# Two products instead of three: high and low activation side by side in one 512-column product, and wider output chunks

## The chip, the cores and the metric

The kernel runs on one core of a Trainium2 chip. The metric is the time of one execution on the device in microseconds (us). Three runs of the kernel before took 2255.21, 2258.01 and 2260.10, with a median of 2258.01.

The engines are TensorE (PE: matrix products; its weight loads are listed as PEld), VectorE (DVE), ScalarE (ACT), GpSimd (POOL), and SyncE (SP), which issues most transfers. TensorE reads SBUF and writes PSUM.

## The reference

Two transformer blocks for one sequence of 256 tokens with 2048 features, in float32. The first block has two layers, the second one layer:

```
for l in range(2):                                  # first block
    h = x @ w_in[l]                                 # 2048 x 8278: queries, keys, values, gates, index
    y_fox = softmax(q k / sqrt(d) + decay, causal) v * silu(gate)      # 6 heads
    y_dsa = softmax over the 64 keys chosen by an index score * silu(gate)   # 6 heads, rotary q and k
    y_mem = softmax(q k_mem) v_mem * silu(gate)     # 4 heads, keys and values from mem @ w_mem_kv[l]
    x = layer_norm(ALPHA * x + concat(y) @ w_out[l])
a = rms_norm(x); proj = a @ w_in_2                  # second block
mixed = concat(attention(q, k, v), conv(u)) @ w_out_2
x = x + rms_norm(mixed)
f = square(relu(rms_norm(x) @ w_ff1)) @ w_ff2       # 2048 -> 8192 -> 2048
x = x + rms_norm(f)
```

Nearly all of the arithmetic is in the products with weights. The kernel makes each in three parts: with w = wh + wl and x = xh + xl, where the h parts are rounded to the type float32r and the l parts are the remainders, it adds wh xh, wh xl and wl xh.

## The kernel before, in words

**Blocks.** All weights stream through SBUF as 734 blocks of 128 partitions by 1024 values (512 KB; some of 512 values). A block g has a place in a ring of four (`RING`): SyncE loads it into `raw`, ScalarE rounds it into `high` (`round_block`, L804), and VectorE or GpSimd writes the remainder into `low` (`low_part`, L449). GpSimd takes every second block in slots 40 to 133 of each layer and all of slots 18 to 83 of block 2. TensorE multiplies the block in `weight_block` (L589 to L618, the product at L617). ScalarE may round block g once TensorE is done with block g - 4.

**Chunks.** `plan` (L91) groups the blocks into chunks, each of which sums over all K-tiles of 128 rows into one of two pairs of PSUM banks (`acc`). Chunks alternate between the pairs, so a chunk waits until the result of the one before the last was read (`acc_released`, L528). There are two kinds. A *flipped* chunk holds 256 output features; the weights are the stationary operand and the activation of 256 tokens moves, so the result has features on the partitions. It takes four blocks of four K-tiles. An unflipped chunk moves the weights and keeps the activation stationary; it has 512 columns (eight blocks of two K-tiles) or 256 columns. Flipped are mk (keys of the memory, 4 chunks in all), mg, fg, fq, fk, mq, iq, dg, dq and dk (26 chunks in each layer), val, gt, q2 and k2 (16 chunks in block 2), and f1 (32). A narrow flipped chunk, nar, is apart in its own bank. Unflipped are the values, the output projections o (in each layer), oa and ob, and f2. The output columns are cut by `COLS` (L76): two chunks of 512 and four of 256. ob sums over 10 K-tiles in five blocks a chunk, two K-tiles in a block.

**Slots.** Each engine goes through the same list of slots, one per block. `slots` (L372) first serves block b, then the side work of slot b - 3 (`LEAD`). The side work is written out by slot number: `ends(b, kinds)` (L423) names the chunk whose last block was b - 1, and then the result is read. ScalarE reads keys, queries, values and gates (`copied_out`, L897; its copy of keys is L913) and the relu (`relu_square`, L1064). VectorE reads what is rotated (`rope`, L1127: first product L1137, parts L1140, last add L1143), the second block's val, gt, q2 and k2 (L1490), and the output sums (`add_residual`, `mix_sum`, `ff_sum`).

**Attention.** `SCORES` and `SCORES2` (L177 to L180) give the slot of each head. In slot b TensorE makes the scores (L641 for memory heads, L644 and L645 for others), VectorE the maximum (L1179 for memory heads), and ScalarE the exponentials. In slot b + 1 VectorE takes the reciprocal of the sums (L1197) and ScalarE the probabilities (L835). In slot b + 2 TensorE transposes them (L655), in b + 3 it multiplies by the values. Within a slot, VectorE's rotation stands ahead of its attention work. The top-k choice takes eight rounds in slots 90 to 97 on VectorE. The depthwise convolution of block 2 is spread over slots 18 to 80, four steps a slot on VectorE (L1462).

**The feed-forward part.** Four rounds, each with 8 f1 chunks and then the f2 chunks; the last three are a loop. The first two f1 chunks of the first round run interleaved, block by block. After the last f2 chunk come its sum (L1416), squares (L894), the root, the gain (L1438) and the last additions, and four transfers out.

Of the kernel before, what the change touches and what calls it, by code (L numbers as in the profile page):

```python
# [54 lines left out]
NQ = 4  # L55
# [20 lines left out]
COLS = [(0, 512), (512, 512), (1024, 256), (1280, 256), (1536, 256), (1792, 256)]  # L76
NC = len(COLS)

# [12 lines left out]
def plan(a):  # L91
# [82 lines left out]
BLOCK2, BLOCK2_SLOTS = LAYER0 + DEPTH * LAYER_SLOTS, 122  # L174
# [3 lines left out]
SCORES |= {62 + 2 * h: ("mem", h) for h in range(HM)}  # L178
# [5 lines left out]
GLU_AT = (17, 25, 41, 49)  # L184
# [27 lines left out]
def build(nc, a, out):  # L212
    by, chunk_at, acc_users = plan(a)
    with ExitStack() as ctx:
# [9 lines left out]
        xh = sb("xh", [P, KT, S], F32R)  # L224
        xl = sb("xl", [P, KT, S], F32R)

        with nc.sbuf_tensor("yhf", [P, KT, S], F32) as yhf:
            pass
        yh = sb("yh", [P, KT, S], F32R)
        with nc.sbuf_tensor("ylf", [P, KT, S], F32) as ylf:  # L230
            pass
        yl = sb("yl", [P, KT, S], F32R)
# [6 lines left out]
        consts = sb("consts", [P, N_CONST])  # L239
        params = sb("params", [P, N_PARAM])  # L240
        small = sb("small", [P, 384])
# [19 lines left out]
        def const(name, *dims):  # L261
            return cut(consts, CONST[name][0], *(dims or (CONST[name][1] - CONST[name][0],)))
# [5 lines left out]
        ident, mask, upto = const("ident"), const("mask"), const("upto")  # L268
# [20 lines left out]
        def mixed_cols(n):  # L289

            col, width = COLS[n]
# [23 lines left out]
        def vec(name, n):  # L315
            sm[name] = small[:, sm_at[0]:sm_at[0] + n]
            sm_at[0] += n
            assert sm_at[0] <= 384
# [16 lines left out]
            v_ready g_ready rot_ready nar_ready flog_in flog_e flog_ln logf_ready wi_ready warm_done ikt_ready slope_ready  # L335
# [7 lines left out]
         logf_ready, wi_ready, warm_done, ikt_ready, slope_ready, cum_ready, decay_ready, rel_ready, rel_used,  # L343
# [18 lines left out]
        def accs(c):  # L362

            b = 2 * (c.acc % 2)
            return acc[:, b:b + 2, 0:256 if c.width == 256 else CW]

# [42 lines left out]
        def sums(kind, *at):  # L409

            return {"o": 0, "oa": 2 * NC, "ob": 2 * NC + 4, "f2": 3 * NC + 4}[kind] + NC * sum(at[:-1]) + at[-1] + 1
# [43 lines left out]
        def _(pe):  # L455
# [72 lines left out]
            def acc_released(c, turn):  # L528
# [22 lines left out]
                else:  # L551
                    pe.wait_ge(sum_ready, NC * turn + sums(*k))
# [36 lines left out]
            def weight_block(g, turn=0):  # L589
# [10 lines left out]
                vh, vl = (yh, yl) if k[0] in ("mk", "mv", "o", "oa", "ob", "f2") else (xh, xl)  # L600
# [4 lines left out]
                for t in range(c.nk):  # L605
                    kt = c.kt0 + c.nk * i + t
                    first, last = i == 0 and t == 0, i == c.n - 1 and t == c.nk - 1
                    for s in range(len(outs)):
                        at = slice(s * P, min(s * P + P, c.width if c.flipped else S))
                        if c.flipped:  # L610
                            products = ((wh[:, t, at], vh[:, kt, :]), (wh[:, t, at], vl[:, kt, :]),
                                        (wl[:, t, at], vh[:, kt, :]))
                        else:
                            products = ((vh[:, kt, at], wh[:, t, :]), (vh[:, kt, at], wl[:, t, :]),
                                        (vl[:, kt, at], wh[:, t, :]))
# [182 lines left out]
        def _(act):  # L798
# [128 lines left out]
            def mem_side(b):  # L927
                name = ends(b, "mk", "mv")
# [10 lines left out]
            for l in range(DEPTH):  # L939
                g0 = LAYER0 + LAYER_SLOTS * l  # L940

                def layer_side(b, l=l, g0=g0):
                    name = ends(g0 + b, "mv", "fq", "fk", "mq", "fv", "dv", "mg", "fg", "dg")
                    if name:
                        copied_out(name)
# [51 lines left out]
            def block2_side(b):  # L997
                name = ends(BLOCK2 + b, "val", "gt", "v2")
# [44 lines left out]
                if b in (98, 103, 108, 113, 118):  # L1043
                    n = (b - 98) // 5
                    act.wait_ge(sum_ready, sums("ob", n))
                    squares(mixed_cols(n), n)
# [4 lines left out]
            squares(mixed_cols(NC - 1), NC - 1)  # L1051
# [27 lines left out]
            def ff_side(b, q, turn=0):  # L1079
                name = ends(FF0 + FF_SLOTS * q + b, "f1")  # L1080
# [13 lines left out]
            for n in range(NC):  # L1094
                act.wait_ge(sum_ready, sums("f2", NQ - 1, n))
                squares(mixed_cols(n), n)
# [4 lines left out]
        def _(dve):  # L1101
# [14 lines left out]

            def low_block(g, turn=0):
# [9 lines left out]
            def rope(k):  # L1127
# [7 lines left out]
                acc_done(c)  # L1135
# [27 lines left out]
            def max_of_scores(l, kind, h):  # L1163
                j = job_no(l, kind, h)
                r = 2 * (j % 4)
                if kind == "fox":
# [3 lines left out]
                                                  in1=mask[:, 0:P], op0=ALU.subtract, op1=ALU.add))  # L1170
                    dve.scalar_tensor_tensor(out=nfox[:, P:3 * P], in0=t[:, 0:S], scalar=cum[:, 1, h:h + 1],
                                             in1=mask[:, P:3 * P], op0=ALU.subtract,
# [61 lines left out]
            def mem_side(b):  # L1234
                if 8 <= b < 24 and b % 2 == 1:
# [25 lines left out]
            for l in range(DEPTH):  # L1261
# [16 lines left out]
                def layer_side(b, l=l, g0=g0):  # L1278
                    name = ends(g0 + b, "iq", "dq", "dk", "o")
# [37 lines left out]
                    if b == TOPK_AT + TOPK // 8 + 1:  # L1317

                        for s, n in ((0, P), (1, S)):
# [3 lines left out]
                                                   mask[:, P * s:P * s + n], ALU.add))  # L1323
# [28 lines left out]
                def select_round(r, l=l):  # L1352

                    both = ((0, P), (1, S))
                    if r == 0:
# [4 lines left out]
                        for s, n in both:  # L1360
                            step(dve.tensor_tensor(iscore[:, s, 0:n], iscore[:, s, 0:n], mask[:, P * s:P * s + n],
# [48 lines left out]
            def ff_sum(name, turn):  # L1410
# [3 lines left out]
                for s in range(ST):  # L1414
                    rows = mixed_cols(n)[:, s, :]
# [3 lines left out]
                dve.wait_ge(sum_ready, NC * turn + sums(*name))  # L1419

            def mix_sum(name):
# [5 lines left out]
                else:  # L1427
                    rows = mixed_cols(name[1])
# [288 lines left out]
```

## Time and profile before

| | |
|---|---|
| runs: lowest, median, highest | 2255.21, 2258.01, 2260.10 us |
| profiled execution: its time | 2256.79 us |
| its span in the trace | 2255.0 us |
| mean granted TensorE clock | 0.991 |
| TensorE products: busy | 2201.1 us (98%) |
| TensorE weight loads: busy | 2088.9 us (93%) |
| VectorE: busy | 1231.1 us (55%) |
| ScalarE: busy | 1058.1 us (47%) |
| GpSimd: busy | 392.3 us (17%) |
| moved by DMA | 395.32 MB, mean 175 GB/s |

Products are pipelined, and the duration shown for one is from its start to its modelled end, so neighbours overlap; the distance between the starts of two is what one costs in a stream. All times of the rows are from one profiled execution and counted from the start of its span.

### The profile page before, as it was taken

Reading aid. Unit: us, or ns where it says so; the run is one execution under the profiler, and the core shown is the slowest. Engines: PE = TensorE matmul, PEld = TensorE weight load, DVE = VectorE, ACT = ScalarE, POOL = GpSimd, SP = SyncE. Lnnn points to the kernel's source line nnn. Section 1 sums busy time; section 2 is a strip of 40 time slices with the busy share of each in tenths; the row PEclk is TensorE's granted clock in tenths of the full one; section 3 lists DMA queues with packets and bytes.
Section 4 is the critical chain, followed back from the end, with each engine's and each line's share of the span. In section 5 each row is a group of like instructions: output and inputs, shape, how many; then the busy total and the mean of one; then the engine's idle time right before and its main releaser. Section 6 shows DMA issues by size and latency. Waiting matters only on the chain.

```text
span 2255.0 us, 38841 instructions
## 1 busy us (share of the span) xinstructions
PE 2201.1 (98%) x16028; PEld 2088.9 (93%) x16028; DVE 1231.1 (55%) x1774; ACT 1058.1 (47%) x1438; POOL 392.3 (17%) x176
## 2 busy tenths in 40 slices
PE   8999999999999999999989999989999999999997
PEld 7999998998889999998979999789899999989987
DVE  4443346765565335855577555665544454444455
ACT  4444454444454554444454445556434434533543
POOL 0000323331000233332007875000000000000000
PEclk9999999999999999999999999999999999999999
DMA  8666545655666555555656655556666665665663
GB/s 272 192 179 184 153 137 163 179 154 181 189 170 179 153 148 167 162 166 167 188 159 197 187 162 166 165 164 181 190 184 183 186 188 170 185 189 175 181 193 124
DMA packets 346186, 395.32 MB, mean 175 GB/s; under 512 B 20336, under 2 KB 295920, under 8 KB 345120
## 3 DMA queue, kind: packets, MB, share of 16 engines
q1 hardware_dynamic: 344368, 383.20, 57.0%
q0 software_dynamic: 1648, 9.64, 1.1%
q8 instruction: 132, 2.16, 0.4%
q14 instruction: 38, 0.31, 0.0%
HBM read 390.70 MB, written 2.10 MB: 174 GB/s over the span
## 4 chain that ended last, share of the span: by engine, by line
PE 94%; DVE 3%; ACT 2%; issue 1%; DMA 0%; DVEq 0%; SPq 0%; ACTq 0%
PE acc L617 88%; ACT high L804 1%; PE tb L559 1%; DVE low L449 1%; PE obank L677 1%; PE sbank L645 1%; PE tb L655 1%; PE sbank L701 0%; PE sbank L617 0%; PE sbank L641 0%; PE sbank L644 0%; PE obank L678 0%; ACT x_nat L972 0%; DVE x_nat L1445 0%; DVE work L1143 0%
## 5 line engine op out<-in xcount | busy, mean ns | idle before, releaser
L804 ACT ACTIVATE high<-raw 128x1024 fp32r<-128x1024 f32 (+1 forms) x734 | 765.9, 1045 | 908.2 <-PE acc L617 891.3
L449 DVE TENSOR_TENSOR low<-raw,high 128x1024 fp32r<-128x1024 f32 (+1 forms) x574 | 709.0, 1236 | 740.6 <-ACT high L804 738.7
L617 PE MATMUL acc<-xh,high 128*128 128x256 f32 x3200 | 919.3, 287 | 10.1 <-DVE low L449 6.9
L617 PE MATMUL acc<-xh,low 128*128 128x256 f32 x3200 | 907.2, 283 | 0.0
L617 PE MATMUL acc<-xl,high 128*128 128x256 f32 x3200 | 907.0, 283 | 0.0
L617 PEld LDWEIGHTS acc<-xh,high 128*128 128x128 f32 x3200 | 615.6, 192 | 13.6 <-DVE low L449 7.3
L617 PEld LDWEIGHTS acc<-xl,high 128*128 128x128 f32 x3200 | 615.6, 192 | 1.1
L617 PEld LDWEIGHTS acc<-xh,low 128*128 128x128 f32 x3200 | 615.5, 192 | 0.0
L449 POOL TENSOR_TENSOR low<-raw,high 128x1024 fp32r<-128x1024 f32 x160 | 384.7, 2407 | 778.7 <-ACT high L804 778.6
L617 PE MATMUL acc<-high,yh 128*128 128x256 f32 (+1 forms) x1384 | 451.7, 326 | 1.5 <-DVE work L1426 1.0
L617 PE MATMUL acc<-high,yl 128*128 128x256 f32 (+1 forms) x1384 | 448.8, 324 | 0.0
L617 PE MATMUL acc<-low,yh 128*128 128x256 f32 (+1 forms) x1384 | 448.7, 324 | 0.0
L617 PEld LDWEIGHTS acc<-high,yh 128*128 128x128 f32 x1384 | 263.4, 190 | 24.2 <-DVE work L1426 1.4
L617 PEld LDWEIGHTS acc<-high,yl 128*128 128x128 f32 x1384 | 263.4, 190 | 21.4
L617 PEld LDWEIGHTS acc<-low,yh 128*128 128x128 f32 x1384 | 263.5, 190 | 20.5
L617 PE MATMUL acc<-high,xh 128*128 128x512 f32 (+1 forms) x320 | 115.8, 362 | 0.7 <-issue 0.7
L617 PE MATMUL acc<-low,xh 128*128 128x512 f32 (+1 forms) x320 | 112.4, 351 | 0.0
L617 PE MATMUL acc<-high,xl 128*128 128x512 f32 (+1 forms) x320 | 112.3, 351 | 0.0
L1462 DVE SCALAR_TENSOR_TENSOR tb<-work,params,tb 128x256 f32<-128x256 f32 x232 | 93.4, 481 | 0.0
L617 PEld LDWEIGHTS acc<-high,xh 128*128 128x128 f32 x320 | 61.5, 192 | 11.0 <-issue 2.7
L617 PEld LDWEIGHTS acc<-high,xl 128*128 128x128 f32 x320 | 61.4, 192 | 8.1
L617 PEld LDWEIGHTS acc<-low,xh 128*128 128x128 f32 x320 | 61.6, 193 | 7.2
(204 smaller groups left out, 1348.8 us busy)
## 6 DMA issues: line engine op xcount, KB each, us to landing
raw<-in_w_in SPq DMA_DIRECT2D x336, 512.0 KB, 3.7
raw<-in_w_ff SPq DMA_DIRECT2D x256, 512.0 KB, 3.8
raw<-in_w_out SPq DMA_DIRECT2D x86, 512.0 KB, 3.9
raw<-in_w_mem_kv SPq DMA_DIRECT2D x32, 512.0 KB, 5.0
raw<-in_w_out SPq DMA_DIRECT2D x20, 256.0 KB, 3.0
x_nat<-in_mem SPq DMA_DIRECT2D x4, 512.0 KB, 7.8
x_nat<-in_x POOLq DMA_DIRECT2D x4, 512.0 KB, 6.3
yhf<-in_ln_gain POOLq DMA_DIRECT2D x2, 1024.0 KB, 5.1
```

The lines of the kernel that those rows point to most:

```text
L449: eng.tensor_tensor(part(low, g), part(raw, g), part(high, g).bitcast(F32), ALU.subtract).then_inc(ready, 1)
L559: ins = pe.transpose(t[:, dt * S + s * P:dt * S + s * P + P], src[:, s, first + dt * P:first + dt * P + P], ident)
L617: ins = pe.matmul(outs[s], stationary, moving, start=first and n == 0, stop=last and n == 2)
L645: ins = pe.matmul(sbank[:, S:2 * S], q[:, h, P:S], k[:, h, :], start=True, stop=True)
L655: ins = pe.transpose(t[:, n * P:n * P + P], sc[:, j % 2, s, kk * P:kk * P + P], ident)
L677: pe.matmul(obank[:, 0:S], v0, t[:, 0:S], start=True, stop=False)
L804: act.activation(part(high, g), part(raw, g), ACT.Copy).then_inc(high_ready, 1)
L1462: ins = dve.scalar_tensor_tensor(out=cv[:, ct, :] if tap == TAPS - 1 else sums_at, in0=src, scalar=w, in1=sums_at, op0=ALU.mult, op1=ALU.add)
```

## The change

In a flipped chunk the first two products, wh with xh and wh with xl, become one of 512 columns. For it `xh` and `xl` (and `yh` and `yl`) are two halves of one tensor, and the moving operand takes K-tile kt of both, in two runs of 256. The result fills a whole bank: the left half holds wh xh, the right half wh xl. The third product, wl with xh, adds to the right half. When the chunk has ended, ScalarE copies the right half of both banks to SBUF (`cross_out`), VectorE adds the copy to the left half in PSUM (`fold`), and only then the result is read. ScalarE's readers of flipped chunks move to the slot after; VectorE's stay in the slot of the fold, but f1's remainder (L1571) moves by two. The memory heads move from slots 62 to 68 to slots 64 to 70, and the gating of the convolution moves by one slot.

Besides, two of the 256-wide output chunks of o and ob are one of 512, and f2 has four chunks of 512 (`FCOLS`). ob has five blocks fewer. Some tables take less SBUF.

```
-COLS = [(0, 512), (512, 512), (1024, 256), (1280, 256), (1536, 256), (1792, 256)]
+COLS = [(0, 512), (512, 512), (1024, 512), (1536, 256), (1792, 256)]
+FCOLS = [(512 * n, 512) for n in range(4)]
-        for n, (col, width) in enumerate(COLS):
+        for n, (col, width) in enumerate(FCOLS):
             add(("f2", q, n), a["w_ff2_2"][0], col, width=width, row0=D * q)
-SCORES |= {62 + 2 * h: ("mem", h) for h in range(HM)}
+SCORES |= {64 + 2 * h: ("mem", h) for h in range(HM)}
-GLU_AT = (17, 25, 41, 49)
+GLU_AT = (18, 26, 42, 50)
-        xh = sb("xh", [P, KT, S], F32R)
-        xl = sb("xl", [P, KT, S], F32R)
+        xhl = sb("xhl", [P, 2, KT, S], F32R)
+        xh, xl = xhl[:, 0], xhl[:, 1]
+        cross = sb("cross", [P, 2, S])[:, :, :]
...
+        def crosses(c):
+            b = 2 * (c.acc % 2)
+            return acc[:, b:b + 2, S:2 * S]
...
                     for s in range(len(outs)):
                         at = slice(s * P, min(s * P + P, c.width if c.flipped else S))
+                        if c.flipped and k[0] != "nar":
+                            b = 2 * (c.acc % 2) + s
+                            both = acc[:, b, :].rearrange("p (h n) -> p h n", h=2)
+                            pe.matmul(both, wh[:, t, at], v[:, :, kt, :], start=first, stop=False)
+                            ins = pe.matmul(acc[:, b, S:2 * S], wl[:, t, at], vh, start=False, stop=last)
+                            continue
...
             def acc_done(c, turn=0):
+                if c.flipped:
+                    act.wait_ge(folded, flip_no(c, turn) + 1)
+                else:
+                    act.wait_ge(block_used, FF_SLOTS * turn + c.blocks[-1] + 1)
+            def cross_out(name, turn=0):
+                c = by[name]
+                n = flip_no(c, turn)
                 act.wait_ge(block_used, FF_SLOTS * turn + c.blocks[-1] + 1)
+                if flips.index(c):
+                    act.wait_ge(folded, n)
+                act.activation(cross, crosses(c), ACT.Copy).then_inc(cross_ready, 1)
...
                 def layer_side(b, l=l, g0=g0):
+                    new = ends(g0 + b, "fq", "fk", "mq", "mg", "fg", "dg", "iq", "dq", "dk")
+                    if new:
+                        cross_out(new)
+                    for name in (ends(g0 + b, "mv", "fv", "dv"), ends(g0 + b - 1, "fq", "fk", "mq", "mg", "fg", "dg")):
+                        if name:
+                            copied_out(name)
...
             def ff_side(b, q, turn=0):
-                name = ends(FF0 + FF_SLOTS * q + b, "f1")
+                new, name = (ends(FF0 + FF_SLOTS * q + b - at, "f1") for at in (0, 1))
+                if new:
+                    cross_out(new, turn)
...
+            def fold(name, turn=0):
+                c = by[name]
+                dve.wait_ge(cross_ready, flip_no(c, turn) + 1)
+                dve.tensor_tensor(accs(c), accs(c), cross, ALU.add).then_inc(folded, 1)
```

## Rows read from the trace of the kernel before

**Rows 1.** The page's shares of the chain that ended last, by engine.

```profile
PE 94%; DVE 3%; ACT 2%; issue 1%; DMA 0%; DVEq 0%; SPq 0%; ACTq 0%
```

**Rows 2.** The page's groups: busy us, mean ns of one | idle before, releaser.

```profile
L804 ACT ACTIVATE high<-raw 128x1024 fp32r<-128x1024 f32 (+1 forms) x734 | 765.9, 1045 | 908.2 <-PE acc L617 891.3
L449 DVE TENSOR_TENSOR low<-raw,high 128x1024 fp32r<-128x1024 f32 (+1 forms) x574 | 709.0, 1236 | 740.6 <-ACT high L804 738.7
```

**Rows 3.** Timeline (start, duration) of TensorE in f1: first and last of 27.

```profile
1559.79 0.28 PE L617 MATMUL acc<-xh,low 128*128 128x256 f32 x1
...
1562.91 0.28 PE L617 MATMUL acc<-xl,high 128*128 128x256 f32 x1
```

**Rows 4.** Timeline of TensorE in f2: first and last of 18.

```profile
1599.98 0.39 PE L617 MATMUL acc<-high,yl 128*128 128x512 f32 x1
...
1603.84 0.39 PE L617 MATMUL acc<-low,yh 128*128 128x512 f32 x1
```

**Rows 5.** Groups by form: products of flipped chunks, and of unflipped 256-wide ones.

```profile
L617 PE MATMUL acc<-xh,high 128*128 128x256 f32 x3200 | 919.3, 287 | 10.1 <-DVE low L449 6.9 <-issue 2.0 <-DVE xl L1551 1.3
...
L617 PE MATMUL acc<-high,yh 128*128 128x256 f32 x848 | 239.9, 283 | 0.0
```

**Rows 6.** Groups by form: operations that read or write PSUM.

```profile
L1462 DVE SCALAR_TENSOR_TENSOR tb<-work,params,tb 128x256 f32<-128x256 f32 x232 | 93.4, 481 | 0.0
...
L1137 DVE TENSOR_TENSOR cb<-acc,consts 128x512 f32<-128x512 f32 x20 | 13.8, 688 | 6.1 <-PE acc L617 6.1
...
L913 ACT ACTIVATE work<-acc 128x512 f32<-128x512 f32 x20 | 11.6, 578 | 0.0
```

**Rows 7.** Timeline of four engines at the rotation in slot 114, layer 0.

```profile
474.17 0.55 PE L655 MATMUL tb<-consts,sc 128*128 128x128 f32 x3 [1.23 <-ACT sc L835]
...
470.15 2.93 DVE L1143 TENSOR_TENSOR work<-cb,ylf 128x512 f32<-128x512 f32 x1
...
469.01 1.04 ACT L804 ACTIVATE high<-raw 128x1024 fp32r<-128x1024 f32 x1
...
470.13 2.40 POOL L449 TENSOR_TENSOR low<-raw,high 128x1024 fp32r<-128x1024 f32 x1 [5.72 <-ACT high L804]
```

**Rows 8.** Timeline around the memory head of slot 68, layer 0.

```profile
327.20 0.69 DVE L1179 TENSOR_REDUCE small<-sbank 128x2 f32<-128x512 f32 x1 [3.02 <-PE sbank L641]
...
332.72 2.84 DVE L1140 TENSOR_TENSOR ylf<-acc,consts 32x512 f32<-32x512 f32 x4
335.60 0.77 DVE L1143 TENSOR_TENSOR work<-cb,ylf 128x512 f32<-128x512 f32 x1
...
324.38 1.04 ACT L804 ACTIVATE high<-raw 128x1024 fp32r<-128x1024 f32 x1
...
331.47 0.91 ACT L835 ACTIVATE sc<-sc,small 128x256 f32<-128x256 f32 x2 [1.37 <-DVE small L1197]
...
333.61 0.60 PE L655 MATMUL tb<-consts,sc 128*128 128x128 f32 x4
```

**Rows 9.** Timeline of ScalarE at the end of the first f1 chunks.

```profile
1530.65 1.06 ACT L804 ACTIVATE high<-raw 128x1024 fp32r<-128x1024 f32 x1
```

**Rows 10.** Timeline of VectorE after the last product.

```profile
2242.37 0.88 DVE L1416 SCALAR_TENSOR_TENSOR work<-acc,small,work 128x256 f32<-128x256 f32 x2 [3.35 <-PE acc L617]
...
2244.71 0.68 DVE L1438 TENSOR_TENSOR work<-work 128x512 f32<-128x512 f32 x1
```

**Rows 11.** Timeline of VectorE and GpSimd in the top-k rounds.

```profile
410.68 2.98 DVE L449 TENSOR_TENSOR low<-raw,high 128x1024 fp32r<-128x1024 f32 x1
...
410.18 2.40 POOL L449 TENSOR_TENSOR low<-raw,high 128x1024 fp32r<-128x1024 f32 x1 [3.36 <-ACT high L804]
```

**Rows 12.** Waits of TensorE: us in total, times, longest us.

```profile
PE acc L617 <- DVE low L449: 7.4, 7, 3.0
...
PE tb L655 <- ACT sc L835: 3.6, 4, 1.2
...
PE sbank L641 <- ACT work L913: 0.6, 2, 0.3
```

More of the change, by code:

```diff
@@ L317, in vec @@
             sm_at[0] += n
-            assert sm_at[0] <= 384
+            assert sm_at[0] <= 304
             return sm[name]
@@ L365, in accs, with flip_no @@
             return acc[:, b:b + 2, 0:256 if c.width == 256 else CW]
+        def crosses(c):
+            b = 2 * (c.acc % 2)
+            return acc[:, b:b + 2, S:2 * S]
+        flips = [c for c in acc_users if c.flipped]
+        def flip_no(c, turn=0):
+            return flips.index(c) + 8 * turn
         def part(buf, g):
@@ L409, in sums @@
         def sums(kind, *at):
-            return {"o": 0, "oa": 2 * NC, "ob": 2 * NC + 4, "f2": 3 * NC + 4}[kind] + NC * sum(at[:-1]) + at[-1] + 1
+            return {"o": 0, "oa": 2 * NC, "ob": 2 * NC + 4, "f2": 3 * NC + 4}[kind] + (NF if kind == "f2" else NC) * sum(at[:-1]) + at[-1] + 1
         def norms(phase, u):
@@ L927, in mem_side @@
             def mem_side(b):
-                name = ends(b, "mk", "mv")
+                new, name = ends(b, "mk"), ends(b, "mv") or ends(b - 1, "mk")
+                if new:
+                    cross_out(new)
                 if name:
@@ L997, in block2_side @@
             def block2_side(b):
-                name = ends(BLOCK2 + b, "val", "gt", "v2")
+                new = ends(BLOCK2 + b, "val", "gt", "q2", "k2")
+                if new:
+                    cross_out(new)
+                name = ends(BLOCK2 + b, "v2") or ends(BLOCK2 + b - 1, "gt")
                 if b in (4, 5, 7, 8):
@@ L1050, in _ @@
             act.wait_ge(sum_ready, sums("ob", NC - 1))
-            squares(mixed_cols(NC - 1), NC - 1)
+            squares(mixed_cols(COLS[NC - 1]), NC - 1)
             root(5)
@@ L1093, in _ @@
                 slots(lambda g: round_block(g, turn), lambda b: ff_side(b, 1, turn), FF0 + FF_SLOTS, FF_SLOTS, 0)
-            for n in range(NC):
+            for n in range(NF):
                 act.wait_ge(sum_ready, sums("f2", NQ - 1, n))
-                squares(mixed_cols(n), n)
+                squares(mixed_cols(FCOLS[n]), n)
             root(7)
@@ L1234, in mem_side @@
             def mem_side(b):
+                new = ends(b, "mk")
+                if new:
+                    fold(new)
                 if 8 <= b < 24 and b % 2 == 1:
@@ L1278, in layer_side @@
                 def layer_side(b, l=l, g0=g0):
+                    new = ends(g0 + b, "fq", "fk", "mq", "mg", "fg", "dg", "iq", "dq", "dk")
+                    if new:
+                        fold(new)
                     name = ends(g0 + b, "iq", "dq", "dk", "o")
@@ L1427, in mix_sum @@
                 else:
-                    rows = mixed_cols(name[1])
+                    rows = mixed_cols(COLS[name[1]])
                     ins = dve.tensor_tensor(rows, rows, accs(c), ALU.add)
@@ L1560, in ff_side @@
             def ff_side(b, q, turn=0):
-                name = ends(FF0 + FF_SLOTS * q + b, "f1", "f2")
+                new = ends(FF0 + FF_SLOTS * q + b, "f1")
+                if new:
+                    fold(new, turn)
+                name = ends(FF0 + FF_SLOTS * q + b, "f2") or ends(FF0 + FF_SLOTS * q + b - 2, "f1")
                 if q == 0 and b == 18:
@@ L1580, in _ @@
             n_sq = 16 + 2 * NC
-            for n in range(NC - 1):
-                gain_rows(n, rowf, n_sq + 2 * (n + 1))
-            ff_sum(("f2", NQ - 1, NC - 1), 0)
-            n_sq += 2 * NC
-            link(row_rms(7, n_sq, rstd4, NC, lambda: gain_rows(NC - 1, rowf, n_sq)))
+            for n in range(NF - 1):
+                gain_rows(FCOLS[n], rowf, n_sq + 2 * (n + 1))
+            ff_sum(("f2", NQ - 1, NF - 1), 0)
+            n_sq += 2 * NF
+            link(row_rms(7, n_sq, rstd4, NF, lambda: gain_rows(FCOLS[NF - 1], rowf, n_sq)))
             for c in range(4):
```

85 lines of the change are left out of this document (43 added, 42 removed).

## The prediction

> **What bounds the kernel now.** I read the busy times first: TensorE is busy for 98% of the span, at a mean granted clock of 0.991, VectorE for 55% and ScalarE for 47%. Then the chain of waits: 94% of it is TensorE [rows 1]. The weight-product line is nearly the whole of it. Then the page's costliest groups: the two helpers that feed it, rounding on ScalarE and the remainder on VectorE, sat idle 908.2 and 740.6 us, ended by a TensorE block (891.3) and by ScalarE (738.7) [rows 2]. So they follow TensorE. Last the timeline inside a block, for what one product costs. 27 products of 256 columns start from 1559.79 to 1562.91, one per 3.12/26 = 0.1200 us [rows 3]; 18 of 512 columns start from 1599.98 to 1603.84, one per 3.86/17 = 0.2271 [rows 4]. At 2.4 GHz, the full level of the clock, the columns alone are 0.1067 and 0.2133. The rest is 13.3 ns and 13.8 ns: a cost of the product, not of its columns. I take 13.3.
>
> **What it removes.** A flipped chunk (weights stationary, activation moving) does three products of 256 columns for each K-tile and each half of its width; afterwards one of 512 and one of 256: the same 768 columns, one product fewer. The plan has 104 flipped chunks besides the narrow ones (4 mk, 26 in each layer, 16 in block 2, 32 f1), each 16 K-tiles by 2 halves: 3328 products fewer. 3200 of them have their row (the other 128 are mk) [rows 5]. Of the unflipped 256-wide output chunks, listed 848 times with yh [rows 5], pairs are merged: one pair in each layer, one in ob, two in each of four f2 rounds. That removes 3 x 2 x (2 x 16 + 10 + 8 x 16) = 1020. In all 4348 x 13.3 ns = **57.8 us**. The slots stay: no DMA of the weights is added and bytes are the same; five ob slots of half size go, which saves some issues and roundings that TensorE covers.
>
> The Trainium skill has a rule against this step: "TensorE: Matmul & The Clock Gate", section "Back-to-back issue gap", gives the warm gap as N/2.4 plus 2.5 ns. By it the step would be worth an estimated 4348 x 2.5 ns = 10.9 us. By this rule the trace disagrees: its gap is 13.3 ns above the columns at 256, five times that.
>
> **What it adds, and what covers it.** 104 ScalarE copies of 128x512 out of PSUM, by the existing key copy 578 ns [rows 6]: 60 us. 104 VectorE adds of a PSUM and an SBUF operand back into PSUM. The trace has no such add. The nearest is the rotation's first product, 688 ns; an upper bound is twice the convolution step, which reads and writes PSUM at 128x256 for 481 ns, so 962 ns [rows 6]; a lower bound is the 578 of a copy. I take 690: 72 us. In a steady stretch both lie inside the idle time of [rows 2], 1.2 and 1.3 us a block against 0.58 and 0.69 in one block of four. If that cover is gone, each copy or add costs its length plus the wait. The consumer on ScalarE runs one slot later and the accumulator's next user comes four blocks (11 us) on, so releases are in time, with one exception below. The strided moving operand (high and low half in two runs) has no row among the products. I take no cost for the second run; the bounds are 0 and a whole product's 13.3 ns.
>
> Where the two helpers are on a chain that TensorE waits for, the additions show. The three places:
>
> *Rotations in the sparse attention* (dq pair 1 and 2, slots 114 and 122, both layers: 4 times). Today VectorE rotates as soon as the maximum is out; the rotation's last add takes 2.93 us, from 470.15 to 473.08, beside GpSimd's 2.40 from 470.13. Then come the reciprocal, ScalarE's probabilities, and the transposes at 474.17 after a stall of 1.23 us [rows 7]. Afterwards the rotation waits for a copy queued behind the rounding that ends 470.05: copy to 470.63, add to 471.35, the rotation's first parts (three adds' worth of 0.69) to 473.5. The last add then meets no GpSimd work and takes some 0.75 (0.77 in [rows 8]), to 474.25: 1.15 us later than 473.08. TensorE also arrives 2 x 0.11 us sooner at the wait. That is 1.4 each, 5.5 us. Queued behind the waiting VectorE add are row sums and the low part; the slack of low parts there is over 4 us, so nothing more. The two scores that wait for dk (slots 119, 127) get 0.15 us each, 0.6 in all.
>
> *Memory attention's last head*, moved from slot 68 to 70, where iq's first rotation stands ahead of the maximum in VectorE's queue. Today that maximum starts 327.20 with the scores; a rotation as it stands elsewhere takes 0.69, then 2.84 from 332.72, then 0.77 to 336.37 [rows 8]. Put in front: rounding ended at 325.4 (0.95 after 324.38, the row overlaps its successor), copy 326.0, add 326.75, rotation to 331.2; so the maximum is 4.0 us late. The transposes at 333.61 have 1.23 of slack over the probabilities (331.47 + 0.91) [rows 8], of which two shorter blocks take 0.3. The stall is 3.1 us in each layer, 6.2 us.
>
> *First two f1 chunks*, which run interleaved. Chunk 0 ends one block before chunk 2 needs its accumulator. Its reader today starts in that block; one slot later it stands behind the rounding that starts at 1530.65 [rows 9] and the copy of chunk 1: 1.06 + 0.58 + 0.58 later, less the small overlaps of such rows, is 1532.8. That rounding is released by the same block's end, by my estimate some 0.25 us before its start, when TensorE is ready too: 2.4 us.
>
> *The tail.* The last sum (0.88) and the gain (0.68) double their width [rows 10], and ScalarE's two squares too. At most that doubles all, some 2.4 us; with a fixed part in each I take 1.5 us.
>
> *Top-k rounds* (slots 90 to 98). VectorE looks full: a low part of 2.98 us at 410.68, every 5.76 us. But it is held by GpSimd's own, 410.18 to 412.58 [rows 11], and needs 1.23. The add fills time that is otherwise spent in this wait: I take zero. What shows it gone: ScalarE's gate copy now waits for VectorE and delays the rounding behind it by some 4 us against a slack of 4.8. If it overran, 1 to 3 us in each layer.
>
> A few stretches can't use the gain (the first blocks wait for transposed input; block 2's for low parts, 7.4 us in 7 waits [rows 12]): 0.8 us. A wait of 0.6 us for mq's copy [rows 12] goes, since mem starts two slots later.
>
> Sum: 57.8 - 5.5 - 0.6 - 6.2 - 2.4 - 1.5 - 0.8 + 0.6 = **41.4 us**. The profiled execution took 2256.79 (span 2255.0 and 1.8 around it), so 2215.4; the runs' median lies 1.2 above it, so **2216.6** on the scale of the runs.
>
> **The rivals.**
>
> *A. The waits cost twice what I count.* For it: the margins at the transposes are small (the sparse ones are 0, the memory one is 1.2), rounding and low parts are strictly queued, the new cross and fold join ScalarE and VectorE in both directions, and every wait on one delays the other. Against: the helpers idle a third of the span [rows 2]. Price: the 16.2 us of waits and tail once more, 2233.
>
> *B. The second run of the moving operand costs a product's worth.* If the 13.3 ns belongs to every run of columns, the flipped part gives nothing: 1020 x 13.3 ns = 13.6 us remain against 17 us of waits and unused gain, less 0.6 gained: 2261, slower than before. It decides from a cost of 12.4 ns per second run on (41.4/3328). For it: no product in the trace has such an operand. Against: the cost is the same at 256 and 512 columns, so it isn't tied to the amount read.
>
> *C. The gap doesn't go with the product*: the stream is held by something that stays, such as the rate at which operands of this type are fed. Then nothing of the 57.8 is gained and the time is 2258.0 + 16.4 = 2274. Against: 512 columns show the same 13.3 ns and not twice it [rows 3, 4], and each product brings its own weight load, which goes too. By the gap in the page of the Trainium skill named above, which would leave 10.9 of the gain, an estimated 2264.
>
> *D. The waits are mostly absorbed*: VectorE's and ScalarE's later queue aligns so that only the tail and f1 cost. 57.8 - 1.5 - 2.4 = 53.9 us: 2204.
>
> **How the numbers follow.** Forecast 0.68 (its own range 2208 to 2226: the adds' bounds of 578 and 962 ns move it by some 2 us, the stalls at half and one and a half times mine by 8), A 0.16, D 0.09, B and C 0.05 together, the change undone by something else 0.02. Range: the own range with D's end and A's, 2204 to 2235, leaves about 2 in 10 out. A measurement here can't tell less than 0.2% (4.5 us) from none. Faster by more: 0.93, within: 0.02, slower: 0.05.
>
> **What would show each step.** The start spacing in a flipped stretch should alternate 0.227 and 0.120, a block of 24 products of 2.88 become 16 of 2.77; if the 512 step is 0.240, B holds. An f1 stretch of 32 blocks takes 3.4 us less, an f2 one 2.6 less. The add's mean should be 0.69 and the copy's 0.58. TensorE's wait for probabilities should rise from 3.6 us to some 15; a new wait for the relu's copy should stand near f1's ninth block; VectorE's mem maximum should start 4 us after the scores. Wrong would be my forecast if the waits for low parts grow beyond 7.4 us, if the clock falls in new stretches, or if the spacing is not as said.

## The result, and the profile after

The changed kernel takes **2237.34 us** (median of 4 runs, 2236.51 to 2241.56) against 2256.61 of the kernel before on the same chip: a ratio of 0.9917, 95% interval 0.9898 to 0.9935. It is 0.8% faster; forecast was 2216.6, range 2204 to 2235. The gain is 19.3 us where 41.4 were forecast. The profiled execution took 2241.56 (span 2239.8, mean granted clock 0.986 against 0.991), and was the slowest of the four.

The page after: busy times, the chain's shares (answering to [rows 1]), and the groups that matter (busy us, mean ns of one | idle before; answering to [rows 2, 5, 6]).

```profile
PE 2168.7 (97%) x11680; PEld 1860.1 (83%) x11680; DVE 1265.3 (56%) x1851; ACT 1104.4 (49%) x1525; POOL 399.3 (18%) x176
...
PE 90%; DVE 5%; ACT 3%; issue 2%; DMA 0%; DVEq 0%; ACTq 0%; SPq 0%
...
L824 ACT ACTIVATE high<-raw 128x1024 fp32r<-128x1024 f32 (+1 forms) x729 | 764.9, 1050 | 843.2 <-PE acc L630 435.8
L629 PE MATMUL acc<-xhl,high 128*128 128x512 f32 x3200 | 1151.6, 404 | 7.4 <-issue 2.4
L464 DVE TENSOR_TENSOR low<-raw,high 128x1024 fp32r<-128x1024 f32 (+1 forms) x569 | 704.4, 1239 | 684.7 <-ACT high L824 682.4
L630 PE MATMUL acc<-xhl,low 128*128 128x256 f32 x3200 | 899.7, 281 | 4.8 <-issue 4.8
...
L1163 DVE TENSOR_TENSOR acc<-acc,cross 128x512 f32<-128x512 f32 x104 | 72.4, 696 | 108.7 <-ACT cross L844 108.1
...
L844 ACT ACTIVATE cross<-acc 128x512 f32<-128x512 f32 x104 | 60.2, 579 | 0.0
```

TensorE still bounds the kernel, the products are 4348 fewer, as foretold, and the helpers still idle under it. The add costs 696 ns (taken: 690), the copy 579 (taken: 578).

TensorE's waits (total us, times, longest us), answering to [rows 12]:

```profile
PE tb L675 <- ACT sc L867: 16.1, 6, 3.5
...
PE acc L629 <- ACT cb L1113: 2.2, 1, 2.2
PE acc L629 <- DVE low L464: 1.9, 5, 0.6
```

The waits are those forecast: "from 3.6 us to some 15" is 16.1, and the relu's 2.2 was put at 2.4. What is off stands in the stream itself. TensorE in f1, as in [rows 3] (start, duration):

```profile
1564.44 0.40 PE L629 MATMUL acc<-xhl,high 128*128 128x512 f32 x1
1564.68 0.28 PE L630 MATMUL acc<-xhl,low 128*128 128x256 f32 x1
1564.79 0.40 PE L629 MATMUL acc<-xhl,high 128*128 128x512 f32 x1
...
1566.56 0.40 PE L629 MATMUL acc<-xhl,high 128*128 128x512 f32 x1
```

Six pairs (512 and 256 columns) in 2.12 us: 353.3 ns for a pair. Forecast was 226.7 + 120 = 346.7. The same in chunk fg of layer 0:

```profile
179.91 0.40 PE L629 MATMUL acc<-xhl,high 128*128 128x512 f32 x1
...
181.99 0.40 PE L629 MATMUL acc<-xhl,high 128*128 128x512 f32 x1
```

Here six pairs take 2.08 us, 346.7 each, as forecast. So the same two instructions run in two rhythms. By the starts of the blocks, 20 chunks run in the fast one (fg, fq 0, fk 0 and fq 1 in both layers, and the eight f1 chunks of the loop's last turn). They save 0.427 us each (11.09 against 11.52 where nothing disturbs them). Nearly all others save 0.21 (11.31), where 32 x 13.3 = 426 ns was forecast. Unflipped streams keep the 227 ns of [rows 4].

The slow rhythm isn't slow in every pair. The 512-column products above start at 1564.44, 1564.79, 1565.14, 1565.50, 1565.85, 1566.20 and 1566.56: two pairs of 0.35 us and then one of 0.36. To the nanosecond, the distances between starts in a slow chunk (dg 1 of layer 0) repeat as 235, 114, 232, 118, 241, 120 ns: pairs of 349, 350 and 361. In a fast chunk (fg 1) they repeat as 231, 112, 233, 117: pairs of 343 and 350. So one pair in three is the slow one.

### The profile page after: what moved, and what is told of

It is laid out like the page before. It is cut to its first block, busy times and chain, and to the rows that moved or that the text cites. A ratio compares the mean times of both kernels' runs of the same rounds, so it can differ in the third digit from the quotient of the medians.

```text
span 2239.8 us, 30403 instructions
## 1 busy us (share of the span) xinstructions
PE 2168.7 (97%) x11680; PEld 1860.1 (83%) x11680; DVE 1265.3 (56%) x1851; ACT 1104.4 (49%) x1525; POOL 399.3 (18%) x176
## 4 chain that ended last, share of the span: by engine, by line
PE 90%; DVE 5%; ACT 3%; issue 2%; DMA 0%; DVEq 0%; ACTq 0%; SPq 0%
PE acc L637 35%; PE acc L629 33%; PE acc L630 16%; ACT high L824 1%; DVE low L464 1%; PE tb L574 1%; PE tb L675 1%; DVE yf L1188 1%; PE sbank L665 1%; PE obank L697 1%; PE sbank L721 1%; PE sbank L637 0%; ACT sc L856 0%; ACT x_nat L1009 0%; PE sbank L664 0%
## 5 line engine op out<-in xcount | busy, mean ns | idle before, releaser
L629 PE MATMUL acc<-xhl,high 128*128 128x512 f32 x3200 | 1151.6, 404 | 7.4 <-issue 2.4
L630 PE MATMUL acc<-xhl,low 128*128 128x256 f32 x3200 | 899.7, 281 | 4.8 <-issue 4.8
L629 PEld LDWEIGHTS acc<-xhl,high 128*128 128x128 f32 x3200 | 606.2, 189 | 161.1 <-issue 9.0
L637 PE MATMUL acc<-high,yhl 128*128 128x512 f32 (+1 forms) x2088 | 608.2, 374 | 1.5 <-DVE work L1480 1.0
L630 PEld LDWEIGHTS acc<-xhl,low 128*128 128x128 f32 x3200 | 608.5, 190 | 1.3
L637 PEld LDWEIGHTS acc<-high,yhl 128*128 128x128 f32 x2088 | 381.5, 188 | 72.1 <-DVE work L1480 1.4
L637 PE MATMUL acc<-low,yhl 128*128 128x512 f32 (+1 forms) x1044 | 388.5, 372 | 0.0
L637 PEld LDWEIGHTS acc<-low,yhl 128*128 128x128 f32 x1044 | 196.8, 188 | 33.6
L637 PE MATMUL acc<-high,xhl 128*128 128x512 f32 (+1 forms) x640 | 176.6, 358 | 0.6 <-issue 0.6
L637 PEld LDWEIGHTS acc<-high,xhl 128*128 128x128 f32 x640 | 114.7, 193 | 19.6 <-issue 2.7
```

The costliest lines, as they stand in the source:

```text
L629: pe.matmul(both, wh[:, t, at], v[:, :, kt, :], start=first, stop=False)
L630: ins = pe.matmul(acc[:, b, S:2 * S], wl[:, t, at], vh, start=False, stop=last)
L637: ins = pe.matmul(outs[s], stationary, moving, start=first and n == 0, stop=last and n == 2)
```

## The experiments

Times are medians, ratios are to the kernel before, measured beside each run on the same chip. After was measured apart from the experiments, of which e1 to e4, e5 to e8 and e9 to e12 were each measured together on one chip. So a difference of medians between these groups is good to a few us only. The code is shown in outline, with lines left out and some put in words.

**e1: one run of 512 columns.** The moving operand is contiguous.

```
-xhl = sb("xhl", [P, 2, KT, S], F32R);  xh, xl = xhl[:, 0], xhl[:, 1]
+xhl = sb("xhl", [P, KT, 2, S], F32R);  xh, xl = xhl[:, :, 0], xhl[:, :, 1]
```

> The changed kernel with one thing different: high and low activation of one K-tile lie side by side in SBUF, so that the 512-column product reads one run and not two runs 16 KB apart. In the changed kernel a pair of products (512 + 256 columns) takes 0.353 us in f1 and 0.346 in fg; 0.347 was predicted. Theory 1, the second run costs some 5 ns: pairs take 0.347 everywhere and the time falls by 3328 x 5 ns = 16 us, to 2221. Theory 2, the cost comes from alternating products of 512 and 256 columns, whatever they read: pairs stay at 0.353 in f1, the time at 2237 within 3.

Measured: 2238.87, ratio 0.9926 [0.9913, 0.9940]. The time is that of after within the intervals, and so are the products' mean durations (404 and 281):

```profile
L631 PE MATMUL acc<-xhl,high 128*128 128x512 f32 x3200 | 1148.1, 402 | 6.9 <-ACT cb L1115 2.2 <-issue 2.0 <-DVE low L466 1.5
L632 PE MATMUL acc<-xhl,low 128*128 128x256 f32 x3200 | 899.5, 281 | 4.3 <-issue 4.3
```

Undisturbed chunks are again 11.09 or 11.31 us. Most are in the same rhythm as in after, but the seven undisturbed f1 chunks in the loop's second turn are fast here and slow there. Besides, some chunks behind a long wait or at the start of a turn differ by 1 to 2 us, as the clock fell in other places. A chunk that is fast in both is equal to 0.01 us. So the second run costs nothing, and rival B's mechanism doesn't show.

**e2: the changed kernel with three 256-column products again.** The copy, the add, the order of the waits and the merged chunks stay; the copy is scaled by zero, since its half holds nothing.

```
-if c.flipped and k[0] != "nar":        # 512 + 256 columns
+if False:                              # 3 x 256 columns into the left half
-act.activation(cross, crosses(c), ACT.Copy)
+act.activation(cross, accs(c), ACT.Copy, scale=0.0)
```

> The changed kernel with the three products of 256 columns as before, all into the left half, and the copy and the add kept (the copy is of the left half times zero, so the sum is unchanged). It keeps all that the change adds and takes away what it gives on the flipped chunks. If the copy, the add and the later readers cost what the prediction says (16 us) and the four or five new half-clock stretches of 3.4 us cost half their length each, the time is 2256.6 - 13.6 + 16.2 + 8 = 2267, slower than before. If the waits are harmless and only the products fall short, it is 2256.6 - 13.6 + 3 = 2246.

Measured: 2262.60, ratio 1.0029 [1.0018, 1.0039], near the first theory's 2267. Its waits are almost those of after:

```profile
PE tb L675 <- ACT sc L867: 14.1, 6, 2.9
```

From here to after, 3328 flipped products go and little else: 25.3 us, so **7.6 ns each**, where I had 13.3 and 44.3 us. The intervals of the two runs leave some 5 us of doubt in this, 1.5 ns a product. The lengths of the chunks say the same by themselves: 20 x 0.427 + 84 x 0.213 = 26.4 us, 7.9 ns each. All the rest together (merging, copies, adds, waits) makes the kernel 0.3% slower than before.

**e3: merging only.** Three products, no copy, no add and no waits for them; chunks, slots and their tables as after.

```
-act.activation(cross, crosses(c), ACT.Copy).then_inc(cross_ready, 1)
-dve.tensor_tensor(accs(c), accs(c), cross, ALU.add).then_inc(folded, 1)
```

> Only the wider output chunks and the moved slots: three products of 256 columns, no copy, no add; ScalarE's readers of flipped chunks still run one slot later and the memory heads stand in slots 64 to 70. Merging is worth 13.6 us by the spacings before; the tail takes 1.5 us of it, the first f1 chunks 1.8, and the memory head behind the rotation 1.8 in each layer. If so the time is 2250. If copy and add are what delays the chains and not the slots, it is 2245; if the merge is worth nothing because the 512-column chunks hold something up, 2257 or more.

Measured: 2249.02, ratio 0.9967 [0.9955, 0.9980]. Its wait for probabilities is nearly that of before:

```profile
PE tb L675 <- ACT sc L860: 4.3, 6, 1.2
PE acc L637 <- ACT cb L1106: 1.7, 1, 1.7
```

So merging with the later slots is worth 6.5 us (2250 was expected, 13.6 of merging less the waits that the slots bring). The 104 copies and adds cost 13.6 (e2 less e3). They cost it where another engine's chain waits for them, not by their length of 60 and 72 us: e2 waits 14.1 us for the probabilities where e3 waits 4.3. The relu's wait is mostly there without them: it comes with the slots.

**e4: attention ahead of the additions.** In slots 70, 114 and 122 VectorE does the reciprocal and the maximum first, then the add and the rotation.

```
+ahead = b in (70, 114, 122)
+if ahead:
+    attention(l, b, SCORES, (0, 3))     # reciprocal, maximum
 ...                                     # add of the halves, rotation
-attention(l, b, SCORES)
+attention(l, b, SCORES, (1, 2) if ahead else (0, 1, 2, 3))
```

> The changed kernel, but on VectorE in slots 70, 114 and 122 of each layer the reciprocal and the maximum of the attention stand ahead of the add and the rotation. Theory of the waits: TensorE's wait for probabilities (16.1 us in 6 waits) falls to under 3, and the half-clock stretches of 3.4 us beside these waits (at 472, 502, 857, 994, 1024) go too, some 1.7 us each: 2237 - 13 - 8.5 = 2215. If the half-clock stretches have another cause, 2224. If the waits only move to the scores that need the rotated keys, over 2230.

Measured: 2221.16, ratio 0.9851 [0.9837, 0.9865], 16 us below after by the medians and 15 by the ratios, for an exchange of order that takes no work away. In the two profiles the four chunks at the rotations are 16.1 us shorter. (Some 2.6 us of the profile's whole gain is another thing: 12 f1 chunks more are in the fast rhythm.) The wait for probabilities fell to 4.8 us and not under 3, as the two memory heads still wait 2.4 each. At the rotation of slot 114 (answering to [rows 7]), first after, then e4 (start, duration [wait]):

```profile
471.02 0.55 PE L675 MATMUL tb<-consts,sc 128*128 128x128 f32 x3 [2.41 <-ACT sc L867]
...
466.33 0.70 DVE L1163 TENSOR_TENSOR acc<-acc,cross 128x512 f32<-128x512 f32 x1 [2.48 <-ACT cross L844]
...
469.23 0.69 DVE L1191 TENSOR_TENSOR work<-cb,yf 128x512 f32<-128x512 f32 x1
469.96 0.17 DVE L1245 RECIPROCAL small<-small 128x2 f32<-128x2 f32 x1
```

```profile
468.96 0.49 PE L675 MATMUL tb<-consts,sc 128*128 128x128 f32 x3
...
465.42 0.17 DVE L1245 RECIPROCAL small<-small 128x2 f32<-128x2 f32 x1 [1.05 <-ACT sc L856]
466.85 0.70 DVE L1163 TENSOR_TENSOR acc<-acc,cross 128x512 f32<-128x512 f32 x1 [1.26 <-ACT cross L844]
```

The reciprocal had everything it needed 1.4 us before the add could start; put first, it fills time in which VectorE waited for the copy, and the transposes don't wait. The wait of 2.41 is near the one I had worked out (1.23 + 1.4 = 2.6). But the stretch from the chunk's first product to the next chunk's grew by 2.55 us from before to after (15.01 to 17.56), and it should be 0.21 shorter: 2.76 to be explained, and the longer wait is 1.18 of it. The rest is the clock. The windows of after, behind the transposes at 471.02 and 502.44, and then of e4 (each line: stretch, its length, busy time and count of PE, PEld, DVE, ACT and POOL, granted clock, DMA share, GB/s):

```profile
471.80:475.20 3.40, 3.40 (x12) 2.83 (x11) 2.11 (x7) 1.73 (x7) 0.00 (x0) 0.53 0.24 38
475.20:480.00 4.80, 4.80 (x30) 4.19 (x29) 2.06 (x2) 2.44 (x4) 2.39 (x1) 1.00 0.36 100
...
502.50:505.50 3.00, 3.00 (x11) 2.62 (x12) 1.56 (x2) 2.57 (x4) 0.30 (x1) 0.50 0.08 27
```

```profile
469.00:472.40 3.40, 3.40 (x24) 3.06 (x22) 3.27 (x8) 0.49 (x1) 0.00 (x0) 1.00 0.56 159
```

After the wait TensorE gets half of its clock (1.2 of 2.4 GHz) for a while. It has 12 instructions in a window of 3.40 us where e4 has 24, and a pair of products takes 0.64 us (from 473.15 to 473.79) in place of 0.35. In before, whose wait there was 1.23 us ([rows 7]), the clock stays up behind it:

```profile
474.80:478.00 3.20, 3.20 (x28) 3.15 (x27) 1.95 (x6) 1.52 (x6) 0.00 (x0) 1.00 0.40 111
```

The Trainium skill ("TensorE: Matmul & The Clock Gate", section "Terms") prices such time at the throttled duration times the share of the clock lost, an estimated 1.7 us for the first of these windows; the trace agrees: 2.76 less 1.18 leaves 1.58.

The profile of e5, the next experiment, has both cases in one execution: its two layers run the same chunk (dk 1) with the same wait of 2.46 us, and it takes 15.94 us in layer 0, where the clock stays up, and 17.50 in layer 1, where it falls.

**e5: products in blocks.** In each block of a flipped chunk the eight 512-column products come first, then the eight 256-column ones.

```
-for t in range(c.nk): for s in range(2): 512 (t, s); 256 (t, s)
+for t in range(c.nk): for s in range(2): 512 (t, s)
+for t in range(c.nk): for s in range(2): 256 (t, s)
```

> The changed kernel; in a block of a flipped chunk the eight 512-column products come first and then the eight of 256 columns. Same products, same columns. One run instead of two changed nothing (2239 against 2237, the same length of each chunk), so two theories are left. Theory 2, alternation: each change of width costs, and only 2 of 16 steps in a block are a change now; a block takes 8 x (0.2267 + 0.120) = 2.77 us everywhere (f1 chunks 11.09 and not 11.31), the time is 2237 - 14 = 2223. Theory 3, a rhythm that is set by what ran before the stretch and not by the order of widths (fg chunks take 11.08 and f1 chunks 11.31 with the same order): f1 chunks stay at 11.31 and the time at 2237.

Measured: 2230.79, ratio 0.9891 [0.9876, 0.9906]. TensorE in f1:

```profile
1562.12 2.00 PE L625 MATMUL acc<-xhl,high 128*128 128x512 f32 x8
1563.96 1.11 PE L629 MATMUL acc<-xhl,low 128*128 128x256 f32 x8
1564.91 1.32 PE L625 MATMUL acc<-xhl,high 128*128 128x512 f32 x5
```

A block takes 2.79 us (1562.12 to 1564.91), against 8 x 353.3 = 2.83 after. All flipped chunks that nothing disturbs are now 11.17 us; after had 11.09 in the fast rhythm and 11.30 or 11.31 in the slow one. That is neither theory's number (11.09 or 11.31). By the intervals the gain over after isn't clear of noise for this run alone; e6, e9 and e10 repeat it, and the lengths say 84 x 0.137 less 20 x 0.08, some 10 us. To the nanosecond, the distances from the first wide product on are 234, 236, 228, 232, 231, 227, 227, 226, then 114, 119 and six of 120: the first five wide products after the narrow ones are the dearer ones, and the later ones are back at the 227 of a pure stream.

**e6: products in pairs.** For each K-tile two of 512, then two of 256.

```
+for t in range(c.nk): 512 (t, 0); 512 (t, 1); 256 (t, 0); 256 (t, 1)
```

> As the block order, but in groups of four: 512, 512, 256, 256 columns. Two of four steps are a change of width. Theory 2: half of the loss is left, f1 chunks 11.20, time 2230. Theory 3: 2237 and 11.31, or 11.09 if this order happens to fall into the faster rhythm.

Measured: 2231.48, ratio 0.9894 [0.9879, 0.9910]; chunks 11.15 us. Four times as many changes of width as in e5, the same time and chunks 0.03 us shorter: the number of changes alone isn't the price. Only strict alternation has the slow rhythm (11.31), and only it has the fast one (11.09), which beats every other order.

**e7: no waits.** e4, with slot 71 in place of 70 (there the add and the rotation of iq's first chunk move behind the reciprocal), and the relu of f1's first chunk right behind its copy.

```
-new = ends(g0 + b, "fq", ..., "iq", "dq", "dk")
+new = ends(g0 + b - (b == 71), "fq", ..., "iq", "dq", "dk")     # nothing in slot 70
+if q == 0 and b in (7, 8):
+    name = new if b == 7 else None       # relu of f1's chunk 0 in slot 7
```

> As attention first (2221), and iq's first add and rotation move behind the reciprocal of slot 71, and the relu copy of the first f1 chunk runs in slot 7 and no longer behind the copy of the second. TensorE's wait for probabilities falls from 4.8 to under 0.6 us and its wait for the relu copy from 2.2 to under 0.5; with the two half-clock stretches near 336 and 850 gone: 2221 - 4.2 - 2 - 2 = 2213. If the half-clock stretches stay, 2215. If the later rotation delays the index scores, over 2218.

Measured: 2217.16, ratio 0.9831 [0.9818, 0.9845], above the 2213 to 2215 that I expected. The wait for probabilities is gone from the list. The relu's is 0.9 us in place of 2.2, not under 0.5, and a new one stands at the memory heads, two of 1.2 us:

```profile
PE obank L694 <- DVE y L1263: 2.4, 2, 1.2
...
PE acc L629 <- ACT cb L1113: 0.9, 1, 0.9
```

In its profile all f1 chunks are in the slow rhythm, where e4 has 19 of them in the other rhythm. That is worth 4.1 us and hides in part what e7 gains over e4.

**e8: e5 and e7 together.** No other edit.

> The block order and the removed waits together. Theory 2: 2213 - 14 = 2199. Theory 3: 2213. The two edits touch different engines, so their gains should add within 3 us.

Measured: 2211.22, ratio 0.9796 [0.9782, 0.9809]. Against after, e7 brings 20.2, e5 6.5, both 26.1 by the medians (19.4, 5.9 and 27.3 by the ratios): the two causes add up within the intervals. The time is between the 2199 and the 2213 expected, as e5's was between its two.

**e9: blocks and one run.** The edits of e5 and e1.

> The changed kernel with each block's eight 512-column products first and its eight 256-column products after them, and with the moving operand of the 512-column products laid out as one run of 512 columns. In the block order alone a flipped chunk takes 11.16 us in all 26 phases, and 346.7 ns per pair of products would make 11.09. Theory A, that the leftover 0.07 us is the price of the two widths following each other (two changes of width per block): 11.16 us again, 2230 to 2232 us. Theory B, that it is the second run of the moving operand, which the alternation had hidden: 11.09 us, 104 x 0.07 = 7 us less, some 2224 us.

Measured: 2233.52, ratio 0.9893 [0.9877, 0.9909]; chunks 11.17 us, as in e5 to 0.01. Theory B falls for this order too.

**e10: blocks in turns.** One block 512 first, the next 256 first.

```
+for wide in ((True, False) if i % 2 == 0 else (False, True)):
+    for t, s in tiles: 512 (t, s) if wide else 256 (t, s)
```

> The changed kernel with blocks in turns: one block runs its eight 512-column products and then its eight 256-column products, the next one the 256-column products first, so that the changes of width are half as many as in the block order (one per block in place of two). Theory A, a price for every change of width: half of the leftover goes, 11.12 to 11.13 us per flipped chunk, some 2227 us. Theory C, that what is left has nothing to do with the change of width (the 512-column steps are 230.7 ns in the mean in the block order, against 226.7 in phases that have only 512-column products): 11.16 us, 2230 to 2232 us, as in the block order.

Measured: 2230.76, ratio 0.9885 [0.9870, 0.9900]. Two blocks in f1:

```profile
1560.76 3.82 PE L628 MATMUL acc<-xhl,high 128*128 128x512 f32 x16
1564.41 2.08 PE L631 MATMUL acc<-xhl,low 128*128 128x256 f32 x16
1566.33 2.91 PE L628 MATMUL acc<-xhl,high 128*128 128x512 f32 x12
```

5.57 us for two blocks, 2.785 each; undisturbed chunks are 11.13, as theory A says, against e5's 11.17. The whole kernel can't tell it: 104 x 0.04 is 4 us, within the intervals. And in e6 more changes of width cost less than in e5, so a fixed price for each change, as A has it, is not shown.

**e12: e7 with blocks in turns.** No other edit.

> The blocks in turns, together with all that took the waits away: row sums and running maximum ahead of the additions on VectorE, the addition of iq's chunk 0 behind them, and f1's relu right behind its chunk's copy. With the block order in place of the turns it measured 2211.2 us, 0.980 of the kernel before. Theory A (price per change of width): 3 to 4 us less, some 2207.5. Theory C: the same 2211. If the turns bring a new wait at the block ends, because a block that opens with 256-column products needs its low parts at once, it is above 2213 and the waits of TensorE on the low parts show it.

Measured: **2208.88**, ratio 0.9789 [0.9776, 0.9802], the best of the case. It beats both kernels: 2.1% below before, some 1.3% below after. It can't be told from e8 (the intervals overlap). Its waits on low parts are 2.0 us together, against 1.9 in after, so the blocks that open with 256 columns bring no new stall of weight:

```profile
PE acc L628 <- DVE low L464: 1.1, 3, 0.6
...
PE acc L631 <- DVE low L464: 0.9, 2, 0.6
```

## Why the prediction was wrong, step by step

The direction was right; the time came out 2.3 us above the range. Step by step, on the scale of the two profiled executions (a chunk's length is the distance between block starts; minus is a gain; the prediction's 41.4 is 41.5 here by rounding):

| step | predicted | found |
|---|---|---|
| 3328 flipped products | -44.3 | -26.4 (20 x 0.427 + 84 x 0.213) |
| merged chunks in o and f2 (960 products) | -12.8 | -12.9 (2 x 1.3 + 4 x 2.57) |
| merged chunk in ob | -0.8 | +0.5 |
| rotations and the scores behind them | +6.1 | +11.5 |
| memory heads, less mq's wait | +5.6 | +7.3 |
| relu | +2.4 | +1.2 |
| tail | +1.5 | +1.5 |
| the rest: unused gain, a longer fall of the clock at v2 (0.8) | +0.8 | +0.5 |
| a fall of the clock at the loop's last turn | 0 | +1.6 |
| sum | -41.5 | -15.2 (profiled: -15.2) |

**The step that failed: what a removed product saves.** "I take 13.3" held for the 1020 unflipped products: a product of 512 columns replaces two of 256, and the stream of equal products keeps its 227 ns. It failed where 512 and 256 alternate: there a removed product saves 13.3 ns in the 20 chunks of the one rhythm and 6.7 in the 84 of the other. I had the two steps from streams of one width each ([rows 3, 4]) and added them; no row of before had the mixture, and I gave it no bound above their sum except in rivals B and C. Measured it is 7.6 ns in the mean (e2 to after), 19 us less than forecast. By the rule of the Trainium skill that I had weighed ("TensorE: Matmul & The Clock Gate", section "Back-to-back issue gap"; 2.5 ns above the columns, given there for a product by itself) it would have been an estimated 8.3 us in place of 25.3; the trace disagrees in the alternating order, and more so in the block order, where 0.35 us a chunk is 10.8 ns a product.

**Stalls: sizes right, their consequence missed.** This is the second part of the shortfall: 18.8 us where 11.7 were forecast. The wait at the rotation was put at 2.6 and is 2.41 and 2.19; at the memory heads it was put at 3.1 and is 3.46 ([rows 8]). TensorE at these waits (start, duration [wait]):

```profile
336.78 0.66 PE L675 MATMUL tb<-consts,sc 128*128 128x128 f32 x4 [3.46 <-ACT sc L867]
...
502.44 0.90 PE L675 MATMUL tb<-consts,sc 128*128 128x128 f32 x3 [2.19 <-ACT sc L867]
...
857.92 1.11 PE L675 MATMUL tb<-consts,sc 128*128 128x128 f32 x4 [3.46 <-ACT sc L867]
```

Missed was the clock behind them. In the profiled execution it fell behind five of the six waits. The two memory heads show its price by themselves: the wait is 3.46 in both layers, the chunk 18.39 us in layer 0, where the clock stayed up, and 19.64 in layer 1, where it fell:

```profile
336.00:340.00 4.00, 3.22 (x20) 2.85 (x21) 1.00 (x3) 3.41 (x6) 2.25 (x1) 1.00 0.45 131
857.50:860.50 3.00, 2.58 (x9) 2.33 (x10) 0.08 (x1) 2.74 (x5) 1.61 (x1) 0.50 0.60 175
```

1.25 us for the same wait. It can be more: in e1 this chunk of layer 1 has the wait of 3.47, then 6.83 us at half clock, and takes 21.14. Over the rotations it is 11.5 less the 5.6 by which the waits grew. I named it as what would make me wrong ("if the clock falls in new stretches") and gave it no price. Where the clock falls differs between profiles with nearly the same waits: behind five of the six here, two in e5, four in e10. Whether it falls more often in the slower of after's four executions is not shown.

**The small ones.** The relu's wait is 2.18 us, as forecast; that the stretch lost only 1.2 is the clock again, which was at half until 1506.1 in before, 6.0 us into f1, and until 1502.4 in after, 2.9 us into it. Merging in ob was worth its 0.8, but the wider sum and squares behind it hold the transposes of x for 5.9 us, where it was 4.6, and 0.5 was lost. For the tail I had counted such a doubling; here I overlooked it. The tail itself is right: its last sum takes 1.41 us in place of 0.88, the gain 1.22 in place of 0.68 ([rows 10]), and with ScalarE's squares that makes the 1.5. Top-k rounds cost nothing, as said: the smallest slack of a low part there went from 0.88 to 0.77 us.

**The rivals.** B is refuted (e1, e9). C, nothing gained by a product fewer, is wrong as a whole; but its thought, that the gap doesn't simply go with the product, is half true in the slow rhythm. A, the waits cost twice, has the nearest time (2233), but that is luck: the two kinds of stalls took 18.8 instead of 11.7, by the clock and not by queues pushing each other, and the larger part of the shortfall isn't in the waits at all. D, the waits absorbed, is refuted by the 16.1 us of waits for the probabilities.

**Open.** What chooses between 346.7 and 353.3 ns in strict alternation, and why one pair in three is the slow one. It isn't the operand's layout (e1), and the orders in pairs and blocks show one length each (e5, e6). It differs between phases of one execution whose instructions are the same, even between turns of one loop: of the three, one is in the fast rhythm in after, two in e1 and e4, none in e7. An own measurement of two widths at different alignments of the stream would be the next step; it wasn't made.

## What to carry to other kernels

The price of an instruction in a stream of equals is not its price in a mixture: before adding the steps of two kinds, give the mixture a bound of its own, and try the order (blocks by kind) when it can be chosen, since here it was worth some 6 us by the times for nothing. When a step adds work to a queue, look for what else stands in that queue behind it with its inputs ready; moving the reciprocal ahead of the add gave back some 16 us, more than the copies and adds had cost (13.6). It could be more because the kernel before has a wait of this kind too (3.6 us, [rows 12]); the same move in the kernel before wasn't run. And a stall of TensorE of 2 to 3.5 us can cost 1.3 to 2.8 us more by the clock that follows, or nothing.

## What the runs showed of the hardware

Unexpected here: a 256-column product every 120 ns and a 512-column one every 227 ns each in its own stream, but 353.3 or 346.7 ns for the pair in strict alternation; 8 and 8 in blocks come to 2.79 us, 16 and 16 to 5.57. The slow alternation is two pairs of 350 ns and one of 361 in turn. A moving operand in two runs costs the same as one of 512 columns (e1: 402 and 404 ns mean). A VectorE add of PSUM and SBUF back into PSUM takes 696 ns at 128x512. And the same wait of 3.46 us was followed by a full clock in one layer and by half of it in the other (e1: in both, for 3.41 and 6.83 us).
